# Retention normalization one chunk later, on alternating accumulator banks

## The reference

```
scores  = (q_n k_n^T) * d_intra            # inside the chunk
o_n     = scores v_n + (q_n * q_dec) state # plus what the state carries
state   = state * c_dec + (k_n * k_dec)^T v_n
ro      = rms(o) * silu(rg)                # per token over the 512 values
ret_out = ro @ ret_w_o
```

## Time and profile before

| | value |
|---|---|
| median of 3 runs | 4113.6 us |
| profiled execution, its own time | 4114.4 us |
| its span (core 5, the slowest) | 4112.9 us |
| spans of the 8 cores | 4087.9 to 4112.9 us |
| mean granted TensorE clock, core 5 | 0.870 of full |
| retention heads, from the first projection | 683 to 1034 us and 1250 to about 1615 us |

### The profile page before, as it was taken

One profiled execution on the slowest core, in us unless ns is written; L12 is line 12 of the kernel. 1 busy time (PEld: TensorE's weight loads), 2 busy tenths in 40 slices (PEclk: granted clock), 3 DMA queues, 4 the chain that ended last, 5 costly groups with the idle time before them and its releaser, 6 DMA issues.

```text
span 4112.9 us, 42170 instructions; the slowest of 8 cores (4087.9 to 4112.9 us)
## 1 busy us (share of the span) xinstructions
PE 3032.6 (74%) x13904; PEld 1278.3 (31%) x13904; DVE 1575.9 (38%) x3116; ACT 1255.8 (31%) x2417; POOL 88.4 (2%) x113
## 2 busy tenths in 40 slices
PE   3999962777796776966766666665976689599993
PEld 2444431333332332422232221321432233244441
DVE  2333345444243443345142251432334424333334
ACT  4111141333212333113645536455112421411112
POOL 0000000000000000000000000000000000000000
PEclk9999986888898887987787787877988999699997
DMA  7322003010212101221001000000231021411102
GB/s 148 44 31 31 6 1 51 1 21 1 41 21 41 21 1 26 37 31 16 1 1 16 1 1 1 1 1 8 44 62 21 1 41 21 72 31 31 32 5 87
DMA packets 91028, 107.84 MB, mean 26 GB/s; under 512 B 3008, under 2 KB 85952, under 8 KB 90688
## 3 DMA queue, kind: packets, MB, share of 16 engines
q0 software_dynamic: 84816, 84.97, 14.2%
q1 hardware_dynamic: 6000, 20.17, 1.4%
HBM read 181.71 MB, written 8.39 MB: 46 GB/s over the span
## 4 chain that ended last, share of the span: by engine, by line
PE 64%; DVE 13%; ACT 10%; issue 7%; DMA 4%; DVEq 1%; ACTq 0%; SPq 0%; POOL 0%; POOLq 0%
PE ps L405 63%; DVE sb_arena L417 7%; ACT sb_arena L414 5%; ACT sb_arena L412 2%; PE ps L408 2%; DVE sb_arena L426 2%; ACT sb_arena L430 1%; DVE sb_HT L417 1%; ACT L414 1%; DMA sb_slot<-ffn_u 1%; DMA sb_X<-x 1%; ACT sb_small L414 1%; DVEq L195 1%; DVE sb_small L435 1%; DMA sb_slot<-app_w 1%
## 5 line engine op out<-in xcount | busy, mean ns | idle before, releaser
L414 ACT ACTIVATE sb_arena<-ps 128x512 bf16<-128x512 f32 (+4 forms) x1224 | 626.1, 550 | 1538.0 <-PE ps L405 1481.4
L405 PE MATMUL ps<-sb_HT,sb_slot 128*128 128x512 bf16 x3328 | 786.5, 390 | 113.0 <-DMA sb_slot<-ret_qk 79.6
L405 PE MATMUL ps<-sb_arena 128*128 128x512 bf16 (+6 forms) x2352 | 664.0, 412 | 262.0 <-DVE sb_arena L417 197.7
L417 DVE TENSOR_TENSOR sb_arena<-sb_arena,ps 128x512 bf16<-128x512 f32 x368 | 253.2, 688 | 935.5 <-PE ps L405 523.4
L405 PE MATMUL ps<-sb_slot,sb_HT 128*128 128x512 bf16 (+1 forms) x2304 | 499.3, 375 | 34.0 <-DMA sb_slot<-diff_qk 28.1
L405 PE MATMUL ps<-sb_slot,sb_arena 128*128 128x512 bf16 x1984 | 473.1, 385 | 55.6 <-DVE sb_arena L417 34.8
L405 PEld LDWEIGHTS ps<-sb_HT,sb_slot 128*128 128x128 bf16 x3328 | 332.7, 100 | 526.7 <-issue 156.3
L405 PEld LDWEIGHTS ps<-sb_arena 128*128 128x128 bf16 (+1 forms) x2352 | 197.2, 102 | 692.2 <-issue 597.2
L408 PE MATMUL ps<-sb_ident,sb_arena 128*128 128x128 bf16 x1184 | 146.5, 268 | 359.4 <-DVE sb_arena L417 193.3
L405 PE MATMUL ps<-sb_arena,sb_ones 128*128 128x512 bf16 (+1 forms) x704 | 281.6, 408 | 160.2 <-ACT sb_arena L414 160.2
L405 PEld LDWEIGHTS ps<-sb_slot,sb_HT 128*128 128x128 bf16 x2304 | 231.5, 102 | 274.0 <-issue 83.5
(11 more groups left out here) (74 smaller groups left out, 1522.1 us busy)
## 6 DMA issues: line engine op xcount, KB each, us to landing
sb_slot<-app_w POOLq DMA_DIRECT2D x32, 512.0 KB, 6.1
sb_X<-x SPq DMA_DIRECT2D x4, 2048.0 KB, 20.4
sb_slot<-w_out POOLq DMA_DIRECT2D x16, 512.0 KB, 5.4
y<-sb_arena SPq DMA_DIRECT2D x16, 512.0 KB, 2.7
sb_slot<-ffn_g POOLq DMA_DIRECT2D x6, 1024.0 KB, 12.3
sb_slot<-ffn_u POOLq DMA_DIRECT2D x6, 1024.0 KB, 11.1
sb_slot<-ffn_d POOLq DMA_DIRECT2D x6, 1024.0 KB, 15.7
sb_arena<-ffn_u POOLq DMA_DIRECT2D x4, 1024.0 KB, 21.7
```

The lines of the kernel that those rows point to most:

```text
L405: P.op("pe", lambda e: e.matmul(out, lhsT, rhs, start=start, stop=stop), r=r, w=w)
L414: P.op("act", lambda e: e.activation(out, in_, func, bias=bias, scale=scale), r=r, w=w)
L417: P.op(eng, lambda e: e.tensor_tensor(out, in0, in1, op), r=r, w=w)
```

## The change

The seven operations that normalize a chunk move into a function post(n, ci, ob). It is called one chunk later: in chunk n, behind the state copies and behind the flush, post runs for chunk n-1. So that chunk n can write its output while chunk n-1 still waits, the output goes to bank 6 for even chunks and to bank 2 for odd ones. The small scalars get a second pair of columns. The flush falls two chunks behind. At the end of each block of four chunks everything is brought up to date: flush of chunk 2 of the block, post of chunk 3.

```diff
--- before.py
+++ after.py
@@ -713,12 +713,25 @@
                         tr(psb[4][:, c * 128:(c + 1) * 128], KT[:, c, cs], r=["KT"], w=[("ps", 4)])
                     tsc(KTOK[:, ci, :], psb[4][:, 0:256], rdec[:, 8 + h:9 + h], None, ALU.mult, None,
                         r=[("ps", 4), "rdec"], w=[("KTOK", ci)])
+                def post(n, ci, ob):
+                    pp = n % 2
+                    rss = small[:, 26 + 2 * pp:27 + 2 * pp]
+                    rf = small[:, 27 + 2 * pp:28 + 2 * pp]
+                    act(T1, ps[ob][:, :], AF.Square, r=[("ps", ob)], w=["T1", ("rss", pp)], accum_out=rss)
+                    tt(rf, rss, rdec[:, 4 + h:5 + h], ALU.mult, r=[("rss", pp), "rdec"], w=[("rf", pp)])
+                    tsc(rf, rf, EPS, None, ALU.add, None, r=[("rf", pp)], w=[("rf", pp)])
+                    act(rf, rf, AF.Sqrt, r=[("rf", pp)], w=[("rf", pp)])
+                    recip(rf, rf, r=[("rf", pp)], w=[("rf", pp)])
+                    tt(rf, rf, rdec[:, h:h + 1], ALU.mult, r=[("rf", pp), "rdec"], w=[("rf", pp)])
+                    stt(RO[pp], ps[ob][:, :], rf, SGt[:, ci, :], ALU.mult, ALU.mult,
+                        r=[("ps", ob), ("rf", pp), ("SGt", ci)], w=[("RO", pp)])
+
+                prev_post = None
                 for ci in range(4):
                     n = tb * 4 + ci
                     t = n
                     cs = slice(ci * 128, (ci + 1) * 128)
-                    ts_ = slice(t * 128, (t + 1) * 128)
-                    rob = RO[n % 2]
+                    ob = 6 if n % 2 == 0 else 2
                     for c in range(2):
                         mm(ps[5][:, 0:128], KT[:, c, cs], QT[:, c, cs], c == 0, c == 1, r=["KT", "QT"], w=[("ps", 5)])
                     tt(SCT, ps[5][:, 0:128], dmask[:, h, :], ALU.mult, r=[("ps", 5), "dmask"], w=["SCT"])
@@ -726,10 +739,10 @@
                         for c in range(2):
                             mm(ps[c][:, :], KTOK[:, ci, c * 128:(c + 1) * 128], VTOK[:, ci, :], True, True,
                                r=[("KTOK", ci), ("VTOK", ci)], w=[("ps", c)])
-                    mm(ps[6][:, :], SCT, VTOK[:, ci, :], True, n == 0, r=["SCT", ("VTOK", ci)], w=[("ps", 6)])
+                    mm(ps[ob][:, :], SCT, VTOK[:, ci, :], True, n == 0, r=["SCT", ("VTOK", ci)], w=[("ps", ob)])
                     if n > 0:
                         for c in range(2):
-                            mm(ps[6][:, :], QT[:, c, cs], Sbf[:, c, :], False, c == 1, r=["QT", ("Sbf", c)], w=[("ps", 6)])
+                            mm(ps[ob][:, :], QT[:, c, cs], Sbf[:, c, :], False, c == 1, r=["QT", ("Sbf", c)], w=[("ps", ob)])
                     if n < 15:
                         for c in range(2):
                             if n == 0:
@@ -738,17 +751,18 @@
                                 stt(Sf[:, c, :], Sf[:, c, :], g128, ps[c][:, :], ALU.mult, ALU.add,
                                     r=[("ps", c), ("Sf", c)], w=[("Sf", c)])
                             cp(Sbf[:, c, :], Sf[:, c, :], r=[("Sf", c)], w=[("Sbf", c)], eng="act")
-                    act(T1, ps[6][:, :], AF.Square, r=[("ps", 6)], w=["T1", "rss"], accum_out=small[:, 4:5])
-                    tt(small[:, 5:6], small[:, 4:5], rdec[:, 4 + h:5 + h], ALU.mult, r=["rss", "rdec"], w=["rf"])
-                    tsc(small[:, 5:6], small[:, 5:6], EPS, None, ALU.add, None, r=["rf"], w=["rf"])
-                    act(small[:, 5:6], small[:, 5:6], AF.Sqrt, r=["rf"], w=["rf"])
-                    recip(small[:, 5:6], small[:, 5:6], r=["rf"], w=["rf"])
-                    tt(small[:, 5:6], small[:, 5:6], rdec[:, h:h + 1], ALU.mult, r=["rf", "rdec"], w=["rf"])
-                    stt(rob, ps[6][:, :], small[:, 5:6], SGt[:, ci, :], ALU.mult, ALU.mult,
-                        r=[("ps", 6), "rf", ("SGt", ci)], w=[("RO", n % 2)])
                     if pending[0] is not None:
                         flush_ro(*pending[0])
-                    pending[0] = (n % 2, t, tb)
+                        pending[0] = None
+                    if prev_post is not None:
+                        post(*prev_post)
+                        pending[0] = (prev_post[0] % 2, prev_post[0], tb)
+                    prev_post = (n, ci, ob)
+                if pending[0] is not None:
+                    flush_ro(*pending[0])
+                    pending[0] = None
+                post(*prev_post)
+                pending[0] = (prev_post[0] % 2, prev_post[0], tb)
             flush_ro(*pending[0])
 
         def diff_tables():
```

## The result

The changed kernel takes 4158 us (4153.2 to 4158.1). The ratio to the kernel before is 1.0105, 95% interval 1.0091 to 1.0118, so 37 to 49 us slower. In some executions one die runs at a lower clock, whatever the kernel: times and ratios here leave them out, and since the profiled execution of the changed kernel had such a die (cores 4 to 7), I read core 2 of the other one and compare it with core 2 of the kernel before. Their spans are 4087.9 us before and 4132.1 after, 44.2 apart, as the two kernels are.

What follows compares the result with a forecast made beforehand. It took a closed ring of 5.39 us per inner chunk across DVE, PE and ACT to bound most of each block; 39 us in the chunks plus 14 for the clock made 53, forecast 4166 us, range 4136 to 4180.

Steps and rivals of the forecast that it cites:

- The second bank alone: Chunk output: alternating banks removes a wait for bank 6 that the chunk does not have, worth 0.
- The sum that hides the bank's last reader: Block's end: the last gated product starts about 2.7 us after the next projection, v's first matmul 6.91 or more after it.
- First chunk: Block's first chunk: no normalization before the next mask product, 2.3 us (1.5 in a head's first block), before 6.78.
- Second chunk: Block's second chunk: now carries the first normalization with the table load, 5.39 plus 1.39, so 6.78 us.
- Third: Block's third chunk: the same 5.39 us plus 0.52 for the flush's copy ahead of the Square, 5.91 us.
- Block end: Last mask product to next projection: transposes wait for the third chunk's gated product, 6.63 us, before 2.08.
- Head end: End of a head: two normalizations in a row, each with its flush, 10.74 us to the projection, before 5.50.
- one ring: Inner chunk: mask product, output matmuls, state copies, Square, small operations, gated product, next mask product; 5.39 us.
- The copy of the flush on the ring: Third chunk: the flush's copy on ACT stands ahead of the Square and costs its slot, 0.52 us, bounds 0 and 0.7.
- The tail: Before the next projection: PE's transposes wait for a gated product; block ends 2.08 to 6.63 us, head ends 5.50 to 10.74.
- The clock: 12 q/k projections behind blocks of their own head: PE idling before them costs 1.2 us each, 14 us in all.
- the fast rival: Inner chunks: normalization really leaves the ring, inner chunk about 3.4 us, kernel 64 us less, 4050; chance 4%.

Runs made afterwards that it cites:

- one-bank run: The opened ring with all output in bank 6 and the gated product of the chunk before ahead of this chunk's output matmuls: 4102.6 to 4106.4 us, ratio 0.9972.
- the kernel before with the drain: The kernel before with the last chunk's flush done at the block's end instead of in the next block's first chunk: 4172.2 to 4175.7 us, ratio 1.0143.
- the changed kernel without it: The changed kernel with the two block-end flushes carried over the next projection, done one per chunk: 4091.5 to 4093.8 us, ratio 0.9946.
- the opened ring: Against the run with carried flushes: Square in its own chunk, Sqrt heading the next, gated product behind its state updates: 3986.5 to 3990.3 us, ratio 0.9689.
- the preload: The opened ring plus one Sqrt of a 128x1 scratch column behind the gate's last Silu: 3971.2 to 3975.7 us, ratio 0.9654.

## Why the prediction was right

It said 4166 and a slowdown of 52; measured are 4158 and 44. The mechanism held, the clock's term was too large. Step by step:

- The second bank alone, worth 0: 0.9998. Right. The one-bank run shows on what it hangs: it holds as long as the order itself keeps a chunk from writing its output before the last one is read out. The sum that hides the bank's last reader was 0.2 us short (0.30 + 0.5 + 2.13 is 2.9 us behind the projection's start, not 2.7); the trace has it at 2.95 (777.88 against 774.93), and nothing hangs on it.
- First chunk 2.3 us (1.5 in a head's first block): 2.69 in the mean of the second and third blocks of core 2, and 1.39. Second chunk 6.78: 6.76, but 6.36 in a head's first block. Third 5.91: 5.88. Block end 6.63: 6.49. Head end 10.74: 10.52. The sum of 39 us for the chunks came out at 40.8 on core 2 and 32 on core 3. These are steps of one ring added in a new order, each from a row, and that is why they hold. That the sum is so near on core 2 is in part luck: the first chunks came out 4 us longer in all, the second chunks and the ends 4 us shorter.
- The copy of the flush on the ring, 0.52: shown by the run that moves it (5.88 to 5.39) and by the changed kernel's timeline.
- The tail, the largest loss: shown from both sides, by the kernel before with the drain (+59 us) and the changed kernel without it (about -65, of which some 8 are the head's end).
- The clock, 14 us: the term that was mis-sized. The 12 projections cost 4.2 us more on core 2, 10.5 on core 3 and 6.5 in the mean of cores 0 to 3, so 0.35 to 0.9 each and not 1.2. The sign that I had named, projections of 8.5 to 9.7 us, did not come on core 2, where they take 8.06 to 8.29. I had taken the price from the single case of the earlier trace rows. What the rows show is that a projection costs its 6.91 us at the full clock and half of the time that it spends at the lower level. Here is one of core 2 of the changed kernel, split where the clock rises (us, PE busy, mean granted clock):

```profile
774.93:777.58 2.65, 2.65 (x9) 0.50 0.00 0
777.58:783.15 5.57, 5.57 (x27) 1.00 0.00 0
```

  It takes 8.22 us, and 6.91 + 2.65 / 2 is 8.23. All 12 of core 2 are like this, with 2.3 to 2.8 us at the lower level. On core 3 six are like it too, but the low part of the other six lasts 4.0 to 5.6 us, behind the same order and the same wait of 3.8 us (4.2 once). One of these:

```profile
1511.27 0.58 PE L408 MATMUL ps<-sb_ident,sb_arena 128*128 128x128 bf16 x4 [3.81 <-DVE sb_arena L426]
...
1511.65:1517.23 5.58, 5.58 (x16) 0.50 0.00 0
1517.23:1521.32 4.09, 4.09 (x21) 1.00 0.00 0
```

  This one takes 9.67 us, the time of the earlier trace rows. And the kernel before had paid already: on core 2 only 2 of its 12 projections ran at the full clock throughout. The wait ahead is a part of the cause at most. In the mean of cores 0 to 3 a projection takes 7.93 us before, 8.71 with the drain alone, 8.47 in the changed kernel, 8.55 with the flush moved behind the normalization, and still 8.25 with the wait gone. Only in the opened ring do they fall to 7.32, and to 6.92 with the preload, where on core 2 the clock is full throughout 11 of the 12. What decides how long the low level lasts stays open. The rule of the Trainium skill (page "TensorE: Matmul & The Clock Gate", section "HAM oscillation — how this bites in real kernels") that each burst behind a repeated gap starts cold agrees with this trace: all 12 projections of core 2 and of core 3 start at the lower level. It was my price for it, 23 us, that was too high, since it took the long low part of the earlier trace rows for each of them.
- The forecast that the fast rival (the ring opened, 4050) would not come by this change held; opened it gave more than I had priced, 3987, mostly since the block's end fell to about 1.7 us where I had put 4.8 (I had left the drain in), and the inner interval to 3.2 where I had put 3.4.

## What to carry to other kernels

Before deferring a stage, write down each engine's order after the change and follow the ring from one iteration's first step to the next one's: an operation that is recorded one iteration later but still stands ahead of the next iteration's first step, on an in-order engine, has left nothing. Deferral also leaves a tail, and a drain in front of work that could have covered it can cost more than the loop gains; carry it over. A second buffer pays only once no order forces the wait that it is to remove: here 0 us in the old order, some 117 in the new.

## What the runs showed that I had not expected

- A chunk without state copies lets the deferred Square start ahead of the mask product, which took 2.8 us off each head's end (10.51 to 7.72) by one moved flush.
- A Sqrt of a single scratch column, 0.20 us, put behind the last Silu takes the 1.28 us table load out of the chunks: 21 us in the kernel before, for one line of code.
- The 12 q/k projections did not follow the distance from the last mask product to them: in the mean of cores 0 to 3 they take 7.93 us behind 1.8 us, 8.25 behind 1.9, 8.47 behind 6.5 and 6.92 behind 1.6. The same burst behind the same wait took 8.2 us on one core and 9.7 on another.
